# State-space stage: u and y copied directly between on-chip buffers, in pieces of 32 KB, in another order of the queues

## What is computed

```python
u = (h @ w_in).reshape(B, S, G, C)
bu_r = einsum('bsgc,gpc->bsgp', u, bbar_r);  bu_i = einsum('bsgc,gpc->bsgp', u, bbar_i)
_, _, xr, xi = associative_scan(combine, (a_r, a_i, bu_r, bu_i), axis=1)
y = einsum('bsgp,gcp->bsgc', xr, c_re) - einsum('bsgp,gcp->bsgc', xi, c_im)
y = gelu(y.reshape(B, S, SSM_WIDTH) + d_skip * u.reshape(B, S, SSM_WIDTH))
val, gate = split(y @ w_glu, 2, axis=-1)
return val * sigmoid(gate)
```

## Time and profile before

| | |
|---|---|
| time, median of 3 runs | 1170.85 us (1170.77 to 1176.56) |
| time of the profiled execution | 1168.75 us |
| its span, first to last instruction | 1167.0 us |
| mean granted clock of PE | 0.987 of full |
| the state-space stage up to the end of its mixed part with `glu` | about 614 to 716 us of the span |
| DMA issues in the stage, for each tile | u out, u in, y out, y in 256 KB each; TM, O and a weight block 512 KB each |

### The profile page before, as it was taken

How to read it: one execution, slowest core, us unless ns; L and a number is a source line. 1 busy time by engine, 2 the same in 40 slices (tenths; PEclk the granted TensorE clock), 3 DMA queues, 4 the chain that set the end, 5 groups by cost and what they waited for, 6 DMA issues and landing times.

```text
span 1167.0 us, 14621 instructions
## 1 busy us (share of the span) xinstructions
PE 1121.3 (96%) x5596; PEld 910.6 (78%) x5596; DVE 795.4 (68%) x1151; ACT 456.4 (39%) x677; POOL 131.6 (11%) x222
## 2 busy tenths in 40 slices
PE   5999999999999999999999989999999999999995
PEld 4777557788888888888787878887888888888874
DVE  5886665988876787678857873556775477635764
ACT  5422553445433543344452223334442244413431
POOL 2837206910000000000000000000000000000000
PEclk9999999999999999999999979999999999999997
DMA  6232001323234332434256862332323323233221
GB/s 220 73 98 92 1 1 54 109 91 127 90 123 149 108 109 91 144 108 135 79 184 180 244 189 92 109 100 81 109 90 101 98 91 106 81 103 108 81 82 72
DMA packets 61749, 125.60 MB, mean 108 GB/s; under 512 B 21744, under 2 KB 30320, under 8 KB 61680
## 3 DMA queue, kind: packets, MB, share of 16 engines
q1 hardware_dynamic: 60528, 120.48, 32.2%
q0 software_dynamic: 1152, 4.19, 1.1%
HBM read 109.97 MB, written 14.68 MB: 107 GB/s over the span
## 4 chain that ended last, share of the span: by engine, by line
PE 84%; DVE 8%; issue 3%; DMA 2%; ACT 2%; DVEq 1%; SPq 1%; ACTq 0%
PE bank L1174 26%; PE bank L1175 26%; PE bank L1176 26%; DVE MX L780 1%; DVE WL L662 1%; PE bank L1389 1%; PE bank L1381 1%; DMA ud_scratch<-UB 1%; DVE Pexp L788 1%; DVE SS L673 1%; PE bank L1340 1%; DMA TM<-kd_scratch 1%; PE bank L1192 1%; PE bank L1187 1%; DVE GL L810 1%
## 5 line engine op out<-in xcount | busy, mean ns | idle before, releaser
L429 ACT ACTIVATE WH<-RAW 128x1024 fp32r<-128x1024 f32 (+1 forms) x184 | 190.2, 1034 | 456.8 <-PE bank L1176 422.0
L1174 PE MATMUL bank<-GH,WH 128*128 128x512 f32 x816 | 323.4, 396 | 14.8 <-DVE GL L700 12.1
L1176 PE MATMUL bank<-GH,WL 128*128 128x512 f32 x816 | 318.9, 391 | 0.0
L1175 PE MATMUL bank<-GL,WH 128*128 128x512 f32 x816 | 318.8, 391 | 0.0
L662 DVE TENSOR_TENSOR WL<-RAW,WH 128x1024 fp32r<-128x1024 f32 (+1 forms) x184 | 223.5, 1215 | 50.5 <-ACT WH L429 50.1
L1174 PE MATMUL bank<-AH,WH 128*128 128x512 f32 x596 | 235.0, 394 | 2.7 <-DVE AL L903 1.6
L1175 PE MATMUL bank<-AL,WH 128*128 128x512 f32 x596 | 232.4, 390 | 0.0
L1176 PE MATMUL bank<-AH,WL 128*128 128x512 f32 x596 | 232.3, 390 | 0.0
L1174 PEld LDWEIGHTS bank<-GH,WH 128*128 128x128 f32 x816 | 154.1, 189 | 50.9 <-issue 13.8
L1175 PEld LDWEIGHTS bank<-GL,WH 128*128 128x128 f32 x816 | 154.2, 189 | 32.5 <-issue 1.2
L1176 PEld LDWEIGHTS bank<-GH,WL 128*128 128x128 f32 x816 | 153.9, 189 | 32.4
(11 more groups left out here) (228 smaller groups left out, 975.0 us busy)
## 6 DMA issues: line engine op xcount, KB each, us to landing
RAW<-in_w_up SPq DMA_DIRECT2D x88, 512.0 KB, 3.4
RAW<-in_w_dn SPq DMA_DIRECT2D x32, 512.0 KB, 3.5
RAW<-in_w_glu SPq DMA_DIRECT2D x16, 512.0 KB, 3.6
RAW<-in_w_dn SPq DMA_DIRECT2D x16, 384.0 KB, 3.0
RAW<-in_w_wo SPq DMA_DIRECT2D x8, 512.0 KB, 3.5
od_scratch<-OO SPq DMA_DIRECT2D x8, 512.0 KB, 2.9
kd_scratch<-KT SPq DMA_DIRECT2D x8, 512.0 KB, 4.6
RAW<-in_w_win SPq DMA_DIRECT2D x8, 512.0 KB, 4.3
```

What stands on the lines that cost most here:

```text
L429: act_(WH[b % RH][:, :n], RAW[b % RW][:, :n], ACT.Copy).then_inc(s_hi, 1)
L1174: mm(out, wh, hi_[:, k, :], start=start, stop=False)
L1175: mm(out, wh, lo_[:, k, :], start=False, stop=False)
L1176: return mm(out, wl, hi_[:, k, :], start=False, stop=stop)
```

## The change

The two DRAM buffers of u and y are gone. SP's queue copies u in eight DMAs of 32 KB for each tile (one per group: 16 partitions of `UB`, 2 KB each, become 128 partitions of `U2`, 256 B each). y goes back likewise, four groups (the even ones) issued by SP and four (the odd ones) by ACT. `u_rows` in SP stands behind the weight load as before, but its wait for the free buffer (`s_Y`, for j of 3 and up) now stands ahead of all of it. `TM` of tile t-1 is issued ahead of y's and has a wait of its own (`s_Y`). The gelu signals its two halves one by one: SP waits for the first (which holds the even groups), ACT for both. ACT issues its four DMAs between `gelu` and `decay`. The waits of PE, DVE and ACT on the landings count 8 DMAs a tile. The declarations of the two DRAM buffers and of their semaphores are gone too.

```diff
@@ SP (block.sync)
-            def u_out(j):
+            def u_rows(j):
                 sp.wait_ge(s_ev, FIRST["win"] + j + 1)
-                sp.dma_start(UD[j], UB[j % 2][:]).then_inc(s_uw, 16)
-
-            def u_in(j):
                 if j >= 3:
                     sp.wait_ge(s_Y, j - 2)
-                sp.wait_ge(s_uw, 16 * (j + 1))
-                sp.dma_start(U2[j % 3][:], cmaj(UD[j])).then_inc(s_ur[j % 3], 16)
-
-            def y_out(j):
-                sp.wait_ge(s_g, j + 1)
-                sp.dma_start(cmaj(YD[j]), Y2[j % 2][:]).then_inc(s_yw, 16)
-
-            def y_in(j):
+                for g in range(GJ):
+                    sp.dma_start(U2[j % 3][:, g, :], UB[j % 2][C * g:C * g + C, :, :]).then_inc(s_ur[j % 3], 16)
+
+            def y_rows(j):
                 if j >= 2:
                     sp.wait_ge(s_act, TILE0["y"] + j - 1)
-                sp.wait_ge(s_yw, 16 * (j + 1))
-                sp.dma_start(YB[j % 2][:], YD[j]).then_inc(s_yr[j % 2], 16)
+                sp.wait_ge(s_g, 2 * j + 1)
+                for g in range(0, GJ, 2):
+                    sp.dma_start(YB[j % 2][C * g:C * g + C, :, :], Y2[j % 2][:, g, :]).then_inc(s_yr[j % 2], 16)
 
             def lags_in(j):
+                if j >= 2:
+                    sp.wait_ge(s_Y, j - 1)
                 k = KD_[j]
...
             for t in range(NJ + 3):
                 if t < NJ:
                     load(FIRST["win"] + 4 + t)
-                    u_out(t)
-                    u_in(t)
+                    u_rows(t)
+                if 3 <= t <= NJ:
+                    lags_in(t - 1)
                 if t >= 3:
-                    y_out(t - 3)
-                    if t - 1 < NJ:
-                        lags_in(t - 1)
-                    y_in(t - 3)
+                    y_rows(t - 3)
@@ ACT (block.scalar)
             def gelu(j):
                 act.wait_ge(s_Y, j + 1)
                 if j >= 2:
-                    act.wait_ge(s_yw, 16 * (j - 1))
+                    act.wait_ge(s_yr[j % 2], 16 * GJ * (j // 2))
                 for gi in range(2):
-                    m = act_(Y2[j % 2][:, gi::2, :], bank[4 + 2 * (j % 2) + gi][:, 0:QJ * NK].rearrange(
-                        "p (a k) -> p a k", k=NK), ACT.Gelu_apprx_tanh)
-                m.then_inc(s_g, 1)
+                    act_(Y2[j % 2][:, gi::2, :], bank[4 + 2 * (j % 2) + gi][:, 0:QJ * NK].rearrange(
+                        "p (a k) -> p a k", k=NK), ACT.Gelu_apprx_tanh).then_inc(s_g, 1)
+
+            def y_rows(j):
+                if j >= 2:
+                    act.wait_ge(s_act, TILE0["y"] + j - 1)
+                act.wait_ge(s_g, 2 * j + 2)
+                for g in range(1, GJ, 2):
+                    act.dma_start(YB[j % 2][C * g:C * g + C, :, :], Y2[j % 2][:, g, :]).then_inc(s_yr[j % 2], 16)
 
             def y_tile(j):
-                act.wait_ge(s_yr[j % 2], 16 * (j // 2 + 1))
+                act.wait_ge(s_yr[j % 2], 16 * GJ * (j // 2 + 1))
...
                 if 3 <= t < NJ + 3:
                     gelu(t - 3)
+                    y_rows(t - 3)
@@ DVE (u_out), PE (inputs, outputs)
-                    dve.wait_ge(s_uw, 16 * (j - 1))
+                    dve.wait_ge(s_ur[(j - 2) % 3], 16 * GJ * ((j - 2) // 3 + 1))
...
-                pe.wait_ge(s_ur[j % 3], 16 * (j // 3 + 1))
+                pe.wait_ge(s_ur[j % 3], 16 * GJ * (j // 3 + 1))
...
-                    pe.wait_ge(s_g, j - 1)
+                    pe.wait_ge(s_g, 2 * j - 2)
```

More of the change, by code:

```diff
@@ L282, in build @@
         KD_ = nc.dram_tensor("kd_scratch", (NJ, P, LQ, C * LQ), F32, kind="Internal").ap()
-        UD = nc.dram_tensor("ud_scratch", (NJ, P, LQ, NK), F32, kind="Internal").ap()
-        YD = nc.dram_tensor("yd_scratch", (NJ, P, LQ, NK), F32, kind="Internal").ap()
         s_raw = [sem(f"raw{i}_loaded") for i in range(RW)]
@@ L302, in build @@
         s_tmr, s_or = [sem("TM0"), sem("TM1")], [sem("O0"), sem("O1")]
-        s_uw, s_ur = sem("ud_written"), [sem(f"U{i}_loaded") for i in range(3)]
+        s_ur = [sem(f"U{i}_loaded") for i in range(3)]
         s_rt, s_E, s_X, s_Y, s_g = sem("RT"), sem("E"), sem("states"), sem("Y"), sem("gelu")
-        s_yw, s_yr = sem("yd_written"), [sem("YB0_loaded"), sem("YB1_loaded")]
+        s_yr = [sem("YB0_loaded"), sem("YB1_loaded")]
         s_sig = sem("sigmoid")
@@ L317, in span @@
             return range(FIRST[name], FIRST[name] + BLOCKS[name])
-        def cmaj(dram):
-            return bass.AP(dram.tensor, dram.offset, [[NK, P], [C * LQ * NK, GJ], [1, NK]])
         @block.sync
```

## The result

| | before | changed |
|---|---|---|
| median of 20 runs, us | 1171.49 (1166.86 to 1176.56) | 1175.43 (1172.12 to 1178.09) |
| ratio of the times, 95% interval | | 1.0037 (1.0024 to 1.0050) |
| the profiled execution / its span, us | 1168.75 / 1167.0 | 1175.26 / 1173.4 |
| mean granted clock in it | 0.987 | 0.984 |

The change makes the kernel slower, by 0.37% in the ratio (the medians are 3.9 us apart), and the interval leaves out no change. 1168.1 us was forecast, in a range of 1163.0 to 1172.5; the time lies above it.

A forecast was written before the change was run, and what follows sets the result against it. PE was taken to bound the mixed part, leaving gains only at the tail: outputs(6) -2.75 us, with clock, y and start at 0 (start up to +1.0), so 1170.85 - 2.75 = 1168.1 us; range 1163.0 to 1172.5.

The forecast's parts named there:

- PE bounds the mixed part, 10.6 us a tile: State-space stage, 630 to 680 us: PE is full at full clock, so shorter ways for u and y gain nothing there.
- I take 0.47: SP's queue: each small copy takes 0.47 us to issue, from loads issued back to back; bounds 0.37 and 1.2.
- I take 0: Start of the stage: block 5's load behind eight copies of u costs nothing, with 1.0 us kept as bound.
- u_rows(7) from the end of `outputs(4)`: SP's queue, tile 7: the eight copies of u start when outputs(4) is done, at 675.6 us.
- U(7) in time: Tail: U(7) is there at 680.9 us, when PE comes free, so inputs(7) waits for nothing.
- TM(6) 0.8 us sooner, landing in 5.5, -2.75: Tail: TM(6) issued at 679.4, not 680.20, lands at 684.9, so outputs(6) starts 2.75 us earlier.
- TM is not sooner: Rival, chance 0.18: TM(6) takes 7.4 us again, gaining 0.85; the start loses 1.0; 1171.0 us.
- The clock falls again at the tail: Tail: PE's 2.9 us without work before outputs(6) drops the clock; everything behind runs as before, only 2.75 us earlier.
- ACT's four copies 1.9 us: ACT between gelu and decay: four issues of y at 0.47 us, 1.9 us in all, delaying y_tile(3) by 1.6.
- XI(6) hidden: Tail: XI(6) comes 1.2 us later, but the first half of outputs(6) at the low clock covers it.
- small copies are dear: Rival, chance 0.12: above 0.77 us a copy, SP's queue sets the period; +15 us, 1186 us at 1.2 us.

The follow-up runs named there:

- e1: Changed kernel with u by DRAM again in two transfers, y direct and TM ahead kept; 1168.61 us, ratio 0.9987 to the kernel before.
- e11: Changed kernel, but u written to DRAM first and the same eight copies made from there; 1192.57 us, one execution.
- e5: Changed kernel, but u copied from 16 partitions to the same 16, in 16 pieces of 2 KB, not 128 of 256 B; 1177.16 us, one execution.
- e3: Changed kernel with u of tiles 0 to 2 by DRAM, tiles 3 to 7 direct; 1171.90 us, ratio 1.0014 to the kernel before.
- e6: Changed kernel with ACT issuing half of u's copies for tiles 0 and 1; 1175.39 us, ratio 1.0040 to the kernel before.
- e7: e1 with a third TM buffer, TM of tile t fetched in step t; 1168.37 us, ratio 0.9982 to the kernel before.
- e2: Changed kernel with y by DRAM again, u direct and TM ahead kept; 1180.78 us, ratio 1.0089 to the kernel before.
- e8: Changed kernel, u and y direct, with a third TM buffer; 1173.36 us, ratio 1.0012 to the kernel before.
- e4: Kernel before with only TM moved ahead of y out, u and y by DRAM; 1179.21 us, ratio 1.0056 to the kernel before.
- e10: e1, two TM buffers, with ACT's issues of y moved behind y_tile; 1167.60 us, ratio 0.9991 to the kernel before.

## Why the prediction was wrong

- **PE bounds the mixed part, 10.6 us a tile: right.** `inputs(2)` to `inputs(5)` follow each other in 10.6 us in both traces; 630 to 680 us is full but for the fall at its head.
- **"I take 0.47" for an issue: wrong, 0.63 to 0.67 in six of the tiles** (5.11 us for eight at tile 7), 0.78 at tile 5 and 0.75 at tile 0, where one took 1.41 (e1's weight load took 1.66 at that place of the stage, so this isn't the copies' own). The nearest row was a load from DRAM; e11 shows 0.455 for those, e5 that the number of pieces doesn't matter. My bounds (0.37 and 1.2) held it.
- **"I take 0" at the start: wrong, 4.15 us, beyond the bound of 1.0.** This is the step that failed, and it is most of the loss: the load and U(0) behind eight issues were put at nothing. It has three parts. U(0): the issues begin where I said (1.93 us behind the zero, said 1.98) and the last lands in 2.15 (said 2.0), but eight take 6.00 us instead of 3.8, and PE waits 1.73. XI(0): the load goes out 3.6 us later than before, not 1.3, and lands 3.82 us after its issue (before 4.7); its copy at 627.03, `lo` and `states(0)` move along, and PE waits 0.70. The clock: behind these two waits it fell to 0.50, which goes with the other 1.65 us of 4.15. I had asked the question of the clock at the tail only. DVE stood 4.29 us, too, for the landing of U(0), before it might fill that `UB` again (before 2.56 us, for PE):

```profile
624.69 1.09 DVE L950 TENSOR_TENSOR UB<-bank,RSTD 128x512 f32<-128x512 f32 x1 [4.29 <-DMA U<-UB]
```

  With u of the first tiles by DRAM (e3) the time at equal clock is back to before, as it is with half of u issued by ACT (e6).
- **u_rows(7) from the end of `outputs(4)`: right** (681.2 and 681.25). **U(7) in time: wrong**, since the last issue starts 1.2 us later than I said (4.5 us behind the first, not 3.3) and lands 3.3 us behind that, not 2.0. PE waits 2.27 us.
- **TM(6) 0.8 us sooner, landing in 5.5, -2.75: wrong, -0.11.** Counted from the end of `outputs(4)`, it is issued after 5.2 us (said 3.8, before 4.6) and takes 6.67. Both together, 1.4 + 1.2, are the missing gain. This is the second term that failed. The rival "TM is not sooner" came nearest, but it put a gain of 0.85 on it and the cause on the landing alone; half of it is the issues.
- **The clock falls again at the tail: right**, though already ahead of `inputs(7)` (1.97 us instead of 1.15), and it came back later: long matmuls are at 0.43 us until 704.8, 11.7 us behind the start of `outputs(6)`, before 10.0. That is most of the 0.91 us.
- **ACT's four copies 1.9 us: 2.78.** XI(6) hidden: right in the changed kernel, as TM is later still; with TM early (e7) it is the next wait.

```profile
681.22 0.66 ACT L607 ACTIVATE Y<-bank 128x256 f32<-128x256 f32 x2 [3.81 <-PE bank L1384]
681.96 2.78 ACTq L615 DMA_DIRECT2D YB<-Y  x4
684.78 0.41 ACT L599 ACTIVATE RT<-s_r 128x252 f32<-128x252 f32 x1 [2.91 <-DVE XI L983]
685.10 1.12 ACT L619 ACTIVATE AH<-YB 128x512 fp32r<-128x512 f32 x1
```

- **Rival "small copies are dear":** its direction came true, but not its mechanism. 0.63 us is under the 0.77 at which the queue would set the period; it hit at the start, where SP has no slack yet. With direct u only e2 shows a queue over 10.6 us a tile, and there y's round trip is part of it. The Trainium skill, "DMA: Bandwidth & Descriptors", section "Rules for kernel authors", says that transfers under 64 KB are mostly overhead; the runs agree, with 0.63 us of issue for 32 KB and at least 2.0 us to land, as long as the quickest 256 KB took the earlier trace rows.

The profiled execution would have taken 1166.0 us by the forecast and took 1175.3. Of the 9.3 us between them 4.15 are the start, 2.64 the gain that TM(6) didn't bring, 0.91 the longer low clock behind it, and 1.44 came ahead of the stage and are not explained.

Of the 3.9 us of the medians about half remains at equal clock (1173.0 against 1171.1); the rest goes with the granted clock, 0.9839 against 0.9864. Shown: direct u carries the loss (e1 against the change, e8 against e7). Supported, not shown: that most of it arises at the start (e3, whose own profile has the start as late as the changed kernel's, by the clock). Argued only: that the short waits amid short matmuls bring the clock down; when it falls differs between executions, and I have one profile of each kernel. e6 leaves this open too: the issues were shared, `inputs(0)` waited for nothing, and the time didn't move.

## What to carry to other kernels

Replacing a round trip by many small copies trades landing time for issue time on an in-order queue: count the issues of everything that stands behind them, and do it at the first tile as well, where nothing has run ahead yet. Take the price of an issue from a row with the same two ends (DRAM or on-chip), or treat it as unknown. When one wait at a tail is shortened, work out the next two in line (here TM, U(7), XI(6)) before counting the gain.

## What was not expected of the hardware

- An issue on SP costs 0.62 to 0.64 us with both ends on the chip in the shortest groups of eight, with 16 or 128 pieces (up to 0.78 in others), and 0.455 from DRAM (up to 0.59). On ACT it was 0.63 to 0.72 in the changed kernel's fours.
- y out (256 KB), issued right behind the 512 KB of `TM` on the same queue, took 4.7 to 6.8 us to y in (e4), instead of 3.7 to 4.1 in the mixed part.
- The clock fell after a single wait of 0.56 us (e3) or 0.82 us (e6) for XI(0), between stretches of short matmuls, while e1 with 0.60, e7 with 0.51 and e10 with 0.62 at the same place kept it, as did the kernel before with 2.38. Idle time alone doesn't tell it.
- The time of the same kernel varies by 11 us between executions (1164.4 to 1175.8 over the 92 of before) and follows its mean granted clock, 1.12 us for 0.001.
